# Two layers in a row without a barrier, the projection of unnormalised x, and rotary halves swapped by transfers

## The reference, cut to what matters

```
def rms_norm(x, g):
    y = x32 * lax.rsqrt(jnp.mean(x32 * x32, axis=-1, keepdims=True) + EPS)
    return (y * g.astype(F32)).astype(x.dtype)

h = rms_norm(x, ln_g)
u = jnp.einsum('bsd,de->bse', h, w_in)           # q, k, v, z of four branches, 4 x 1024 gate logits
o_sb = stick_breaking_attention(q_sb, k_sb, v_sb)
o_fx = forgetting_attention(rms_norm(q_fx), rms_norm(k_fx), v_fx, log_sigmoid(f_fx + b_forget))
o_dl = dilated_mixture(rope(rms_norm(q_dl)), rope(rms_norm(k_dl)), v_dl)     # 12 heads, 3 patterns
o_mm = memory_cross_attention(rms_norm(q_mm), rms_norm(km), vm)              # km, vm from mem
merged = sum over branches of sigmoid(gate) * ((o * silu(z)) @ w_branch)
x = x + merged @ w_out

def rope(x):                                      # halves of 32 features of each head of 64
    x1, x2 = x32[..., :half], x32[..., half:]
    return jnp.concatenate([x1 * cos - x2 * sin, x2 * cos + x1 * sin], axis=-1)
```

## Time and profile before

| what | value |
|---|---|
| median of the runs | 1473.55 us |
| the profiled execution | 1473.23 us, of which the span from first to last instruction is 1471.4 us |
| PE busy | 1366.6 us (93%), mean granted clock 0.966 |
| POOL / ACT / DVE busy | 708.7 / 688.0 / 506.0 us |
| first layer's first dense matmul | 23.29 us |
| second layer's first dense matmul | 744.08 us |
| last dense matmul of the second layer | 1454.67 us |

### The profile page before, as it was taken

One profiled execution on the slowest core, in us unless ns is written; L12 is line 12 of the kernel. 1 busy time (PEld: TensorE's weight loads), 2 busy tenths in 40 slices (PEclk: granted clock), 3 DMA queues, 4 the chain that ended last, 5 costly groups with the idle time before them and its releaser, 6 DMA issues.

```text
span 1471.4 us, 18405 instructions
## 1 busy us (share of the span) xinstructions
PE 1366.6 (93%) x6264; PEld 1051.6 (71%) x6264; DVE 506.0 (34%) x762; ACT 688.0 (47%) x1278; POOL 708.7 (48%) x586
## 2 busy tenths in 40 slices
PE   6998999998999999999979899999889999999997
PEld 4766867865667788887757578777656668888876
DVE  5687231233331122222248843213332301222232
ACT  4554522476444544444335534226654445444432
POOL 5556631343332366676355566213432424676662
PEclk8999999998999999999989989999899999999998
DMA  5422321121222144444243224112112222344432
GB/s 177 124 74 65 102 63 37 36 51 43 51 58 56 46 110 104 108 109 115 72 124 101 65 72 108 35 31 51 44 49 52 58 57 64 99 110 108 104 115 96
DMA packets 206974, 115.68 MB, mean 79 GB/s; under 512 B 8212, under 2 KB 200980, under 8 KB 206872
## 3 DMA queue, kind: packets, MB, share of 16 engines
q1 hardware_dynamic: 206872, 114.42, 29.6%
HBM read 108.10 MB, written 6.29 MB: 78 GB/s over the span
## 4 chain that ended last, share of the span: by engine, by line
PE 49%; issue 18%; POOL 14%; DVE 8%; ACT 7%; DMA 2%; SPq 1%; ACTq 0%; POOLq 0%; DVEq 0%
PE dense L715 32%; PE score L715 9%; POOL w_lo L1596 7%; PE acc L715 3%; POOL normed L1629 3%; ACT w_hi L1118 3%; DVE turned L1438 3%; PE out L715 2%; DMA w_raw<-in_w_in 2%; POOL o_norm L1637 1%; POOL inv_den L1637 1%; PE turn L715 1%; DVE negmax L1481 1%; POOL dk_lo L1641 1%; PE turn L840 1%
## 5 line engine op out<-in xcount | busy, mean ns | idle before, releaser
L1596 POOL TENSOR_TENSOR w_lo<-w_raw,w_hi 128x512 fp32r<-128x512 f32 (+1 forms) x398 | 481.9, 1219 | 611.4 <-ACT w_hi L1118 595.7
L715 PE MATMUL dense<-h_hi,w_hi 128*128 128x512 f32 x1168 | 507.7, 435 | 29.9 <-DVE h_lo L1327 15.9
L715 PE MATMUL dense<-h_lo,w_hi 128*128 128x512 f32 x1168 | 466.2, 399 | 0.0
L715 PE MATMUL dense<-h_hi,w_lo 128*128 128x512 f32 x1168 | 466.0, 399 | 0.0
L715 PEld LDWEIGHTS dense<-h_hi,w_hi 128*128 128x128 f32 x1168 | 225.9, 193 | 116.4 <-DVE h_lo L1327 19.0
L715 PEld LDWEIGHTS dense<-h_lo,w_hi 128*128 128x128 f32 x1168 | 226.0, 194 | 50.6 <-issue 11.5
L715 PEld LDWEIGHTS dense<-h_hi,w_lo 128*128 128x128 f32 x1168 | 225.3, 193 | 50.8
L1118 ACT ACTIVATE w_hi<-w_raw 128x512 fp32r<-128x512 f32 (+1 forms) x398 | 225.9, 586 | 53.9 <-PE dense L715 51.0
L1333 DVE TENSOR_SCALAR sig<-sig 128x512 f32<-128x512 f32 x64 | 48.3, 755 | 262.2 <-ACT sig L1173 262.2
L1247 ACT ACTIVATE probs<-score 128x512 f32<-128x512 f32 (+1 forms) x48 | 27.2, 575 | 110.4 <-PE score L715 110.3
L1382 DVE COPY raw<-dense 128x512 f32<-128x512 f32 (+1 forms) x48 | 31.8, 663 | 118.3 <-PE dense L715 118.3
(11 more groups left out here) (280 smaller groups left out, 1939.5 us busy)
## 6 DMA issues: line engine op xcount, KB each, us to landing
w_raw<-in_w_in SPq DMA_DIRECT2D x296, 256.0 KB, 2.9
w_raw<-in_w_out SPq DMA_DIRECT2D x32, 256.0 KB, 2.8
x_scratch<-v_dil SPq DMA_DIRECT2D x16, 256.0 KB, 3.6
w_raw<-in_w_mem_kv SPq DMA_DIRECT2D x16, 256.0 KB, 2.8
v_dil<-x_scratch SPq DMA_DIRECT2D x16, 256.0 KB, 2.7
silu_z<-in_mem SPq DMA_DIRECT2D x4, 512.0 KB, 4.0
w_raw<-in_w_br_dil SPq DMA_DIRECT2D x16, 128.0 KB, 2.3
w_raw<-in_w_br_sb SPq DMA_DIRECT2D x16, 128.0 KB, 2.2
```

Of the source, the lines that this page charges most:

```text
L715: return nc.tensor.matmul(o, lhsT, rhs, start=start, stop=stop, skip_group_check=True)
L1596: pool.tensor_tensor(w_lo[:, n % SPLIT_SLOTS, c], w_raw[:, n % RAW_SLOTS, c], f(w_hi[:, n % SPLIT_SLOTS, c]), ALU.subtract).then_inc(w_lo_ ...
```

## The change

There are three parts.

**Layers in a row.** The hardware loop becomes plain code: the two layers are written out one behind the other, and no semaphore is cleared. Counts go on (`Signal.now`, `ago=1` for the layer before). Weight items are numbered through both layers, so the second layer's items follow the first one's in the same slots. Transposing x out becomes three steps `out` between the last output tiles; the transfers out are eight of 256 KB.

**Unnormalised x.** The steps `h` are gone. `h_hi` and `h_lo` are made from x times the gain alone, in the first layer while the tokens arrive (256 tokens at a time), in the second from each new tile of x right after its output tile. `x_sum` moves into the first dense tile of a layer, and its result `x_rstd_row` is multiplied in by DVE as it evicts each bank of the projection (all q, k, v, z, f, g tiles). For normed tiles ACT now squares `raw` and copies nothing. A gate's bank, which ACT read for its exponential, is evicted by DVE first; the rest of the sigmoid moves to post2. In the first layer the squares are summed by ACT over the rows of the tokens.

**Rotary.** The four crosswise copies on DVE become four transfers of 32x512 (64 KB each), issued by ACT in post3. There are two places for the swapped halves, in turns; `normed` stays one buffer. sin, cos and sum move to post4, the rounding to a new post5.

```diff
-                rope = waiting[4]
+                for r in waiting[4]:
+                    add("post4", r)
+                waiting[5] += waiting[4]
                 waiting[4] = []
                 while len(waiting[2]) >= lag and not (...):
                     waiting[3].append(waiting[2].pop(0))
                     add("post2", waiting[3][-1])
-                for r in rope:
-                    add("post4", r)
             if h == len(t.items) - 1:
                 add("post1", t)
                 for r in waiting[3]:
                     add("post3", r)
+                for r in waiting[5]:
+                    add("post5", r)
...
-    for kt in range(KT):
-        add("h", kt)
-    add("h_end")
-    dense([new(kind, DIL, i) for kind in "qk" for i in range(6)], lag=2)
+    dense([new(kind, DIL, i) for kind in "qk" for i in range(6)], [("room",), ("x_sum",)] + [("room",)] * 14, lag=2)
...
-    dense([new("o", None, dt) for dt in range(KT)])
-    for j in range(EARLY):
-        add("early", j)
-    add("x_sum")
+    dense([new("o", None, dt) for dt in range(HALF + 1)])
+    add("out", 0)
+    dense([new("o", None, dt) for dt in range(HALF + 1, KT - 1)])
+    dense([new("o", None, KT - 1)], [("room",), ("out", 1)])
+    add("out", 2)
...
-                for n in range(RAW_SLOTS):
-                    load_item(n, (l + 1) % DEPTH, w_next_in)
-                sp.wait_ge(w_next_in, 16 * RAW_SLOTS)
-                sp.wait_ge(layer_done, 4)
-                sp.sem_clear(range(layer_sems[0].num, layer_sems[-1].num + 1))
-                sp.sem_inc(layer_go, 1)
... ACT
+                        act.activation(h_hi[:, kt, :], xT[:, kt, :], ACT.Copy,
+                                       scale=ln_all[:, (l + 1) * KT + kt:(l + 1) * KT + kt + 1]).then_inc(h_hi_ready.sem, 1)
...
-                        act.activation(square[:, square_ring.slot(t.n), 0:t.width], bank_[:, 0:t.width], ACT.Square)
-                        act.activation(raw[:, raw_ring.slot(t.n), 0:t.width], bank_[:, 0:t.width], ACT.Copy)
+                        act.wait_ge(*raw_ready.of(t.n))
+                        act.activation(square[:, square_ring.slot(t.n), 0:t.width], raw[:, raw_ring.slot(t.n), 0:t.width],
+                                       ACT.Square).then_inc(squared.sem, 1)
...
+                    elif kind == "post3" and s[1].rope:
+                        act.wait_ge(*normed_ready.of(t.n))
+                        wait(act, (turned_ring, spare_ring)[i].before(t.n))
+                        for q in range(4):
+                            act.dma_start(turned_of[i][32 * q:32 * q + 32, :], normed[32 * (q ^ 1):32 * (q ^ 1) + 32, :])\
+                                .then_inc(halves_in[i], 16)
... DVE
+                        elif t.kind == "g":
+                            dve.tensor_tensor(sig_place(t), bank_[:, :], x_rstd_row[:, :], ALU.mult).then_inc(g_kept.sem, 1)
+                        elif t.of_h:
+                            dve.tensor_tensor(raw[:, raw_ring.slot(t.n), :], bank_[:, :], x_rstd_row[:, :], ALU.mult)\
+                                .then_inc(raw_ready.sem, 1)
...
-                        for q in range(4):
-                            last = dve.tensor_copy(turned[32 * q:32 * q + 32, :],
-                                                   normed[32 * (q ^ 1):32 * (q ^ 1) + 32, :])
+                    elif kind == "post4":
+                        dve.wait_ge(*halves_there(t))
+                        dve.tensor_tensor(swapped, swapped, rope[:, 1, :], ALU.mult).then_inc(sin_done.sem, 1)
+                        dve.wait_ge(*sin_done.of(t.n))
+                        dve.wait_ge(*cos_done.of(t.n))
+                        dve.tensor_tensor(swapped, normed[:, :], swapped, ALU.add).then_inc(rope_done.sem, 1)
```

More of the change, by code:

```diff
@@ L84, in raw, with of_h @@
         return self.kind not in ("g", "y", "o")
+    @property
+    def of_h(self):
+        return self.kind not in ("mk", "mv", "y", "o")
 def plan_layer():
@@ L215, in plan_layer @@
     dense([new("y", FOX, KT - 1)])
-    dense([new("o", None, dt) for dt in range(KT)])
-    for j in range(EARLY):
-        add("early", j)
-    add("x_sum")
-    assert all(t.kind == "o" for t in waiting[2])
-    steps = [s for s in steps if s[0] != "split" or s[1] < len(stream)]
+    dense([new("o", None, dt) for dt in range(HALF + 1)])
[3 more added lines that the diff above has]
+    add("out", 2)
+    assert all(t.kind == "o" for t in waiting[2]) and not any(waiting[i] for i in (3, 4, 5))
     return steps, tiles, stream
 class Signal:
+    now = 0
     def __init__(self, sem, keys):
@@ L449, in build @@
         ones_set = signal("ones_set", [0])
-        raw_ready = signal("raw_ready", posts(1, lambda t: t.raw and not t.normed))
+        raw_ready = signal("raw_ready", posts(1, lambda t: t.raw))
+        f_raw = signal("f_raw", [0])
+        g_kept = signal("g_kept", posts(1, lambda t: t.kind == "g"))
         sig_exp = signal("sig_exp", posts(1, lambda t: t.kind in ("z", "g")))
@@ L727, in three_twice, with out_bank @@
                         mm(o, wl if part == 2 else wh, xl if part == 1 else xh, start=start and part == 0)
[L729 to L735 removed]
+            def out_bank(i):
+                return (R[0], R[1], O, A0)[i]
             pe.wait_ge(ident_in, 16)
@@ new lines, in first_square, with first_high @@
+            def first_square(i):
+                act.wait_ge(x_tok_in[i], 16)
+                if i:
+                    act.wait_ge(first_squares, i)
+                act.activation(flat(square[:, :, :]), token_stage(i), ACT.Square, accum_out=first_ms[:, i:i + 1])\
+                    .then_inc(first_squares, 1)
+            def first_high(u):
+                act.wait_ge(x_placed, 4 * u + 4)
+                c = slice(u * MEM, (u + 1) * MEM)
+                for kt in range(KT):
+                    act.activation(h_hi[:, kt, c], xT[:, kt, c], ACT.Copy, scale=ln_all[:, kt:kt + 1]).then_inc(first_h_hi, 1)
@@ L1103, in log_exp @@
+            act.preload_act_table_set("natural_log_exp_and_others")
+            first_square(0)
+            first_split(0)
+            first_square(1)
+            act.wait_ge(params_in, 16 * DEPTH)
+            first_high(0)
+            first_square(2)
+            first_split(1)
+            first_high(1)
+            first_square(3)
+            first_split(2)
+            act.wait_ge(setup, 2)
+            for l in range(DEPTH):
+                Signal.now = l
                 def log_exp(t):
@@ new lines, in constants_in_place @@
+            def constants_in_place():
+                dve.wait_ge(const_in, 16 * CONST_LOADS)
+                dve.wait_ge(setup_pool, 5)
+                stage = flat(probs[:, :, :])
+                for l in range(DEPTH):
+                    last = dve.tensor_scalar(qk_g[:, 6 * l:6 * l + 6:2], qk_g[:, 6 * l:6 * l + 6:2], HD ** -0.5, None, ALU.mult)
+                last.then_inc(setup, 1)
+                dve.tensor_copy(rconst[:, :, :].rearrange("p a b -> p (a b)"), stage[:, 0:8 * P]).then_inc(setup, 1)
+                dve.tensor_copy(pick[0:NH, :], stage[0:NH, 8 * P:8 * P + NH]).then_inc(setup, 1)
+                dve.wait_ge(setup, 5)
```

583 lines of the change are left out of this document (271 added, 312 removed).

## The result

The changed kernel is slower by 0.8%, a small but clear difference: 1486.65 us in the median of 4 runs (1485.83 to 1488.38) against 1474.83 of the kernel before in 4 runs beside it. The ratio is 1.0083, 95% interval 1.0065 to 1.0101. The prediction said 1465.0 and faster, with a range that ended at 1486, so it was wrong in sign and just missed in range. Its own second rival, the long ring, is what happened (a ring is here the closed chain of work and waits from one tile's `normed` to the next; its length is the time per tile).

What follows compares the result with a forecast made beforehand. PE was busy 93% of the span, so gains lay in its stands: the 7.79 us rotary ring and the seams. Start -9.5, between layers -17.5, end -6.2, ring +23, gates +2 gave -8.2 on 1473.2: 1465.0 us, range 1440 to 1486.

Steps and rivals of the forecast that it cites:

- Rival 2: Rotary stage: slow issues or late landing make a step 9.4 to 10; slower from 9.37, 1487 us at 10.0; chance 0.20.
- the walk through the ring: Rotary stage, from a tile's eviction: 0.73 + 1.5 + 2.5 + 4.3 = 9.0 us a tile, +23 us for both layers.
- the start: Kernel start: PE begins near 16.4 instead of 23.29, first `normed` near 35.6 instead of 45.1: -9.5 us, give or take 2.
- the gates: Gate stages: DVE's cap stands ahead of the eviction of y, 16 places at 0 to 0.5 us, taken as +2.
- the attention: Attention stages: ACT loses a copy per normed tile, DVE gains an eviction per tile; -8 to +4 us, taken as 0.
- the transposes: Second layer's output stage: 28 transposes now stand between dense matmuls with nothing hiding them, +3.6 us.
- The bounds: Rotary ring: 8.6 us with issues of 0.28, 10.2 with slow issues that wait, 7.8 if ACT issues cost next to nothing.
- rival 1: Rotary stage: the ring is short, issues on ACT cheap; 1456 us at 8.6, 1438 at 7.8; chance 0.25.
- rival 3: Between layers: the second layer still waits, its 17.5 us gain falls to about 5, time 1477 us; chance 0.06.
- rival 4: Rotary stage: PE's clock stays at 1.2 GHz, a tile takes 12 us, PE is the bound, 1531 us; chance 0.02.
- Seam: Between the layers: PE goes on without a stop, first `normed` at 748.4 against 765.9: -17.5 us.
- end: Last add to span's end: about 5.8 us instead of 15.6, -9.8; net -6.2 with the transposes' +3.6.

Runs made afterwards that it cites:

- e3_copies_act_cos: Changed kernel with DVE copies for the transfers, q and k evicted by ACT without x_rstd, cosine ahead of the weight item: 1436.0 us, 0.9747 of the kernel before.
- e2_sp_issue: Changed kernel with the same four 32-row transfers issued by SP between its weight loads instead of by ACT: 1439.5 us, 0.9775 of the kernel before.
- e2_copies: Changed kernel with the swap done by four DVE copies instead of transfers, all else kept: 1450.7 us, 0.9847 of the kernel before.

## Why the prediction was wrong

- **Failed step.** The term that failed is the second of the walk through the ring: "ACT: the square of tile n is started, then four issues. [...] I take 0.37, near a weight load's 0.38, and that the issues run while the square does: 1.5." They do run beside the square (60.16 and 60.24), but four take 2.44 us (0.51 for the first, 0.61 for each of the others, 0.03 between), so the term is 2.44 and not 1.5. The mechanism was right and a size was off. The other terms measured 0.86 (0.73 predicted), 2.57 (2.5) and 4.35 (4.3). Together the ring is 10.2 instead of 9.0; +0.94 of the 1.2 is this one term, +0.13 the hand-over from eviction to square.
- **Its weight.** 22 steps make +49.8 us of the longer ring, against the +23 predicted: 26.8 us of error. All the other pieces together came to -36.7 (13.1 - 49.8), against -31.2 predicted, so 5.5 us of it are given back. That is luck: the start was worse than predicted, the gates, the attention and the transposes were better. Without these 5.5 the time would be near 1492.
- **The bounds.** Issues on SP took 0.28 to 0.51. The rows were of transfers of other shapes, and none was of a transfer of 32 rows from one buffer on the chip to another. Nor were they all that the trace had. At the start of the kernel before, where SP's issues follow each other without a wait, some take 0.65:

```profile
4.40 0.65 SPq L659 DMA_DIRECT2D headsum<-in_c_square  x1
5.10 0.65 SPq L660 DMA_DIRECT2D rope<-in_c_rope  x1
```

  Four at 0.65 would have given 2.6 and a ring of 10.1. I took the value of a weight load, and thought of a ring of 10.2 only together with a second mishap (issues that wait for the square). In truth an issue of 0.61 lies outside the rows shown and brings 10.2 without the mishap; the range had been cut at a ring of 9.95. Whoever extends rows to an engine and a shape that they do not show should let the bound go beyond them.
- **Rival 2** said 1487 at a ring of 10.0, decided from 9.37, and named the place. It gave it 0.20. It was right on the place, and half right on the cause: neither the wait for the square nor a slow landing (2.0, hidden: last issue starts near 62.07) was needed. That its time fits (1486.7) is partly luck: by its own price of 2.2 us for each 0.1, a ring of 10.2 gives 1491, and the 5.5 us above make the rest.
- **Rivals 1, 3 and 4.** The short ring of rival 1 did not come: no issue on ACT took less than 0.47 us. A ring of 7.35 came only with SP as the issuer. (With four issues at 0.2 together the walk gives 9.0 - 1.5 + 0.2 = 7.7, where the prediction has 7.8.) The layers do follow each other without a wait. The clock was low for part of the stage, as predicted:

```profile
50.00:150.00 100.00, 77.87 (x245) 53.13 (x244) 54.94 (x50) 37.71 (x66) 43.97 (x31) 0.81 0.35 88
```

  This window of the kernel after shows a granted clock of 0.81. Matmuls of 0.63 us stand beside ones of 0.39, after PE has stood for its bank (1.88 us at 60.12). The kernel before has 0.97 in the same window. That it cost little here, as the ring without PE in it was longer, is argued and not shown: no run holds the clock and changes the rest. For it: the ring changed by what the issues give, whether the clock was 0.97 (one transfer), 0.91 (two), 0.81 (four) or 0.82 (eight) in this window.
- **Seam and end** were right to 0.2 us (-17.6 against -17.5; -10.0 against -9.8). The start was 2.4 us too hopeful: PE began at 18.08 and not at 16.4, which is 1.7 of it. The second layer's output stage, with transposes in it, is 2.2 us longer than before, and 3.1 longer than the first layer's in the same kernel (50.2 and 47.0), so the transposes themselves cost nearer to the 3.6 than the table's 2.2 says. The gates show no cost in the window that was read (PE 50.00 of 50 us busy from 550 on, where I had put +2), and the stretch from the last `normed` to the output stage gained some 3 us over both layers.

## What to carry to other kernels

Moving work from a compute engine to transfers is not free for the issuer: count transfers, not bytes, at some 0.6 us each on the issuing sequencer (0.5 for the first of a row), and ask what is queued behind them on that engine. Put them on an engine whose queue holds nothing of the same chain (SP here: 1439 against 1487 us for identical transfers). And when two orders of the same work are compared on DVE and POOL, price each DVE operation by what POOL runs beside it, since 0.69 to 0.75 us became 1.65 to 1.87 here, and one moved step cost 27 us.

## What the runs showed of the hardware

- Issue time hardly depends on the rows, but on the place in a row of issues. On ACT the first takes 0.51 us (16 and 32 rows) or 0.47 (64 and 128), each that follows 0.61 to 0.62 (16, 32 and 64 rows); on SP 0.51 and 0.59 (32 rows). Some take up to 1.70, and why stays open. Data land 2.0 us after the start of an issue of 32 or 64 KB, 2.3 to 2.4 with 128 or 256 KB.
- Issues on ACT run while its own activation does (square 60.16 to 60.79, issues from 60.24), but the next activation waits for the last issue (1.93 us).
- A DVE operation with two f32 operands from SBUF takes 0.69 alone. If POOL has started before, it ends some 0.55 us after POOL's operation does (`w_lo` 58.62 to 60.34, `normed` 59.24 to 60.89 in e3_copies_act_cos), and if DVE has started first, POOL's is the one that grows (1.84 instead of 1.28 at 73.28 in e2_sp_issue, with `normed` 0.75 at 73.22). The Trainium skill's page "SBUF — State Buffer" (SBUF: two separate sides) says that the pair of ports that the two engines share is an exclusive lock, held for the whole instruction by whoever starts first. The trace agrees but for some 0.14 us: an operation of 0.69 that were blocked whole would end 0.69 after POOL's and not 0.55. The rule would have priced the sum's 1.69 in the earlier trace rows as a wait for `w_lo`'s end and not as a slow operation.
- The Trainium skill's page "SBUF — State Buffer" (SBUF: two separate sides) counts DVE operations with only one SBUF input among these only in some modes. The trace has both kinds. The eviction from the bank, with its one SBUF input, took 0.67 to 0.69 us in all 80 places of the kernel after. A copy of 32x512 took 0.42 alone, but in the kernel before the first of each four, which found `w_lo` running, took 1.40 in the median; so about 1 us of the 2.69 in the earlier trace rows is this wait, and four copies take 1.72 in e2_copies.
